# Differential attention, one head after another: v's transposes, norm sums and evictions placed one step later, and the ALiBi slopes moved from the bias table into q

## What is computed

```python
def diff_attention(q, k, v, lam, slopes):
    """q, k (b,s,h,2,d); v (b,s,h,e); lam scalar; slopes (h,).
    out_t = sum_s [softmax1 - lam*softmax2]_{ts} v_s, both maps with ALiBi."""
```

## Time and profile before

| | us |
|---|---|
| median of 3 runs | 4327.98 (4327.98 to 4328.1) |
| the profiled execution | 4328.54 |
| its span in the trace | 4326.8 |
| the attention stage in it, PE's first `av` to the last `ya` | 1778 to 2627, so 849 |
| from the first scores of head 1 to those of head 7 | 1928.4 to 2540.8: 612.4, or 102.1 a head |

### The profile page before, as it was taken

The page is one execution under the profiler, slowest core; times in us unless marked ns, Lnnn a source line. Parts: engine busy times, 40 slices in busy tenths (PEclk is TensorE's granted clock), DMA queues, the critical chain, the costliest instruction groups (busy, mean ns, idle before and its releaser), DMA issues.

```text
span 4326.8 us, 48830 instructions
## 1 busy us (share of the span) xinstructions
PE 3819.9 (88%) x20470; PEld 3154.3 (73%) x20470; DVE 2173.4 (50%) x2809; ACT 1657.8 (38%) x2217; POOL 528.7 (12%) x437
## 2 busy tenths in 40 slices
PE   6989999999987989788888877999888998879988
PEld 5768888787865777666666656977777777658988
DVE  3444343434464657355454443357777777732222
ACT  4323222121134555456566552144444444431122
POOL 0000011000002425000000000012222222200002
PEclk9989999999998989899999997999999999989999
DMA  2002021111111010100000004121111111142111
GB/s 87 30 25 79 30 73 46 42 49 49 49 50 40 30 40 20 49 25 25 25 25 25 25 17 158 40 75 33 40 39 40 35 49 44 47 178 78 40 40 64
DMA packets 196399, 211.31 MB, mean 49 GB/s; under 512 B 7944, under 2 KB 171733, under 8 KB 196181
## 3 DMA queue, kind: packets, MB, share of 16 engines
q1 hardware_dynamic: 190420, 187.22, 13.6%
q10 hardware_dynamic: 5760, 20.97, 1.2%
HBM read 174.62 MB, written 33.55 MB: 48 GB/s over the span
## 4 chain that ended last, share of the span: by engine, by line
PE 65%; DVE 16%; ACT 11%; issue 5%; DMA 2%; POOL 0%; SPq 0%; ACTq 0%; DVEq 0%; POOLq 0%
PE pd L211 56%; PE pq L211 7%; DVE t L2374 2%; ACT t L2322 2%; ACT t L311 2%; DVE t L320 2%; DVE t L2696 1%; PE pd L354 1%; PE pq L354 1%; DVE t L3099 1%; DVE t L2688 1%; DVE t L1785 1%; DVE t L2392 0%; DVE t L3084 0%; ACT L2358 0%
## 5 line engine op out<-in xcount | busy, mean ns | idle before, releaser
L211 PE MATMUL pd<-t 128*128 128x512 f32 (+2 forms) x15920 | 3132.6, 357 | 139.8 <-DVE t L599 43.4
L211 PEld LDWEIGHTS pd<-t 128*128 128x128 f32 x15920 | 2582.8, 193 | 628.6 <-issue 172.6
L211 PE MATMUL pq<-t 128*128 128x128 f32 (+5 forms) x3222 | 575.0, 341 | 155.2 <-DVE t L2374 37.7
L211 PEld LDWEIGHTS pq<-t 128*128 128x128 f32 (+2 forms) x3222 | 400.4, 186 | 286.7 <-issue 69.1
L311 ACT ACTIVATE t<-t 128x2048 fp32r<-128x2048 f32 (+2 forms) x134 | 241.6, 1804 | 754.1 <-PE pd L211 696.4
L320 DVE TENSOR_TENSOR t<-t 128x2048 fp32r<-128x2048 f32 (+2 forms) x134 | 295.5, 2206 | 385.9 <-ACT t L311 385.9
L354 PE MATMUL pd<-t 128*128 128x128 f32 x832 | 137.5, 318 | 108.6 <-DVE t L2392 32.3
L1385 DVE TENSOR_TENSOR t<-pd,t 128x512 f32<-128x512 f32 x256 | 171.6, 689 | 122.8 <-PE pd L211 122.8
L354 PEld LDWEIGHTS pd<-t 128*128 128x128 f32 x832 | 116.3, 165 | 134.9 <-DVE t L2392 32.1
L2322 ACT ACTIVATE t<-t 128x1024 f32<-128x1024 f32 x128 | 146.2, 1144 | 94.0 <-DVE t L2379 93.9
L2696 DVE SCALAR_TENSOR_TENSOR t<-t 128x1024 f32<-128x1024 f32 x120 | 178.6, 1488 | 0.3
(11 more groups left out here) (283 smaller groups left out, 2800.3 us busy)
## 6 DMA issues: line engine op xcount, KB each, us to landing
t<-in_w_in_dram SPq DMA_DIRECT2D x97, 512.0 KB, 4.9
t<-in_w_mlp_dram SPq DMA_DIRECT2D x32, 1024.0 KB, 5.3
t<-in_w_out_dram SPq DMA_DIRECT2D x20, 1024.0 KB, 5.1
t<-in_w_in_dram SPq DMA_DIRECT2D x16, 1024.0 KB, 5.4
t<-ym_scratch ACTq DMA_DIRECT2D x24, 512.0 KB, 7.2
t<-in_x_dram SPq DMA_DIRECT2D x16, 512.0 KB, 7.2
x_scratch<-t SPq DMA_DIRECT2D x16, 512.0 KB, 2.8
ym_scratch<-t SPq DMA_DIRECT2D x16, 512.0 KB, 2.6
```

Of the source, the lines that this page charges most:

```text
L211: ins = e.matmul(out, l, r, start=(first and j == 0), stop=(last and j == n - 1), skip_group_check=True)
```

## The change

There are two parts.

First, the slopes. `bias` is set once to -|distance|, and the factor goes to q: q's high and low parts are multiplied by 2^(h-2), and DVE's scores instruction scales by 2^-(h+1). Each is a power of two. L2316 is gone, and one multiplication at the stage's start is new.

Second, the order. The square comes ahead of the copy; the sum of squares, logarithm, exponential, gate and the write of a half are taken out of their place behind `AV` and put one or two tiles later (`*_att_ms`): the first half's at tile 4 (PE, ACT) and 5 (DVE, SP) of the head, the second half's at tile 0 and 1 of the next head. In `vg` both `av` come first, then `avT` with `ag` for each half. On ACT and DVE each eviction of `vg` and `qk` is one step later than the product. `tmp` has four tiles instead of two. `att_stage` spells out the weave with `vg` as a string of letters.

```diff
-    tmp = ring(ph, 2, [128, 512])
+    tmp = ring(ph, 4, [128, 512])
...
         for th in range(2):
             fm(e, u, 0, th, 2, "av", h, th)
             yield
+        for th in range(2):
             b = e.take(PD, "avT", h, th)
             e.wait_ge(*at["avc", h, th])
             transposed(e, b, [tmp.of("avc", h, th)[:, tile(j)] for j in range(4)]).then_inc(
                 *at.inc("pe", "avT", h, th, free=("avc", h, th)))
-            yield
-        for th in range(2):
             fm(e, u, 128, th, 2, "ag", h, th)
-            yield
-        pe_done(u)
+            if th == 1:
+                pe_done(u)
+            yield
+            yield
...
+    def owed(h, tt):
+
+        return (h, 0) if tt >= 4 else (h - 1, 1)
...
+    def act_att_ms(e, h, tt):
+        h, th = owed(h, tt)
+        if h >= 0:
+            q = tmp.of("osq", h, th)
+            e.wait_ge(*at["oms", h, th])
+            e.wait_ge(*at["epsc"])
+            e.activation(q[:, :], PD.of("oms", h, th)[:, :], ACT.Ln, scale=1.0 / 128, bias=epsc[:, 0:1]).then_inc(
+                *at.inc("act", "oln", h, th, free=("oms", h, th)))
+            e.wait_ge(*at["oln", h, th])
+            e.activation(q[:, :], q[:, :], ACT.Exp, scale=-0.5).then_inc(*at.inc("act", "ors", h, th))
...
-        e.mul(bias[:, :], bias[:, :], -4.0 if h == 0 else 0.5).then_inc(*at.inc("act", "bias", h))
...
-                next(a)
-                next(d)
-                weave((islice(a, 18), 18), (d, 5))
+                for who in "dada" "aaaaad" "aad" "aaaad" "ad" "aaaaa":
+                    next(a if who == "a" else d, None)
                 weave((a, 9), (qk(e, h + 1), 4))
```

More of the change, by code:

```diff
@@ L2177, in act_att_setup @@
         e.wait_ge(*at["dist"])
[L2178 removed]
+        e.activation(bias[:, :], bias[:, :], ACT.Abs).then_inc(*at.inc("act", "abs_dist"))
+        e.wait_ge(*at["abs_dist"])
+        e.mul(bias[:, :], bias[:, :], -1.0).then_inc(*at.inc("act", "bias"))
     def pe_att_vg(e, h):
@@ L2203, in act_att_vg @@
             e.copy(vT[:, :], PD.of("av", h, th)[:, :]).then_inc(*at.inc("act", "avc", h, th, free=("av", h, th)))
-            yield
+            if th == 0:
+                yield
+        for th in range(2):
             e.wait_ge(*at["avT", h, th])
@@ L2217, in act_att_vg @@
                 *at.inc("act", "agt", h, th, free=("ag", h, th)))
-            yield
+            if th == 0:
+                yield
+    QK4 = [(1, 0), (1, 1), (0, 0), (0, 1)]
     def pe_att_qk(e, h):
         u = pe_unit(e, W2in, [(2592 + h * 128, 128), (3616 + h * 128, 128)])
[L2222 to L2226, removed]
-    def act_att_qk(e, h):
-        act_unit(e)
[L2230 to L2242, removed]
@@ new lines, in pe_att_qk, with out_ @@
+        for m, th in QK4:
+            fm(e, u, m * 128, th, 2, "aqk", h, m, th)
+            if (m, th) == QK4[3]:
+                pe_done(u)
+            yield
+    def act_att_qk(e, h):
+        def out_(m, th):
+            sl, b = half(th), PD.of("aqk", h, m, th)
+            e.wait_ge(*at["aqk", h, m, th])
+            if h:
+                e.wait_ge(*at["scores", h - 1, 7, 1])
+            if m == 0:
+                e.mul(QS[0][LO, sl], b[LO, :], 2.0 ** (h - 2)).then_inc(*at.inc("act", "qk0", h, m, th))
+                e.mul(QS[1][HI, sl], b[HI, :], 2.0 ** (h - 2)).then_inc(*at.inc("act", "qkh", h, m, th))
+            else:
+                e.copy(KS[0][LO, sl], b[LO, :]).then_inc(*at.inc("act", "qk0", h, m, th))
+                e.copy(KS[1][HI, sl], b[HI, :]).then_inc(*at.inc("act", "qkh", h, m, th))
+                e.copy(KS[0][HI, sl], b[LO, :]).then_inc(*at.inc("act", "kc", h, th))
+                e.copy(KS[1][LO, sl], b[HI, :]).then_inc(*at.inc("act", "qkh", h, m, th))
+            at.also("act", ("aqk", h, m, th))
+        act_unit(e)
+        yield
+        for i in range(4):
+            out_(*QK4[i])
+            if i < 3:
@@ new lines, in dve_att_qk, with pe_att_ms @@
+        dve_unit(e)
+        yield
+        for i in range(4):
+            out_(*QK4[i])
+            if i < 3:
+                yield
+    def owed(h, tt):
+        return (h, 0) if tt >= 4 else (h - 1, 1)
+    def pe_att_ms(e, h, tt):
+        h, th = owed(h, tt)
+        if h >= 0:
+            b = e.take(PD, "oms", h, th)
+            e.wait_ge(*at["osq", h, th])
+            mms(e, b[:, :], [(ones[:, :], tmp.of("osq", h, th)[:, :])]).then_inc(*at.inc("pe", "oms", h, th))
+    def act_att_ms(e, h, tt):
+        h, th = owed(h, tt)
+        if h >= 0:
+            q = tmp.of("osq", h, th)
[5 more added lines that the diff above has]
+            e.activation(q[:, :], q[:, :], ACT.Exp, scale=-0.5).then_inc(*at.inc("act", "ors", h, th))
@@ L2262, in pe_att, with sp_att_ms @@
+    def sp_att_ms(e, h, tt):
+        h, th = owed(h, tt)
+        if h >= 0:
+            r = (8 + h) * 128
+            e.wait_ge(*at["oy", h, th])
+            e.dma(YM[r:r + 128, half(th)], AB[h % 2][0][:, half(th)], "ya", h, th)
     def pe_att(e, h):
@@ L2353, in act_att @@
                 e.wait_ge(*at["AV", h, th])
[L2354 to L2362, removed]
+                e.activation(q[:, :], b[:, :], ACT.Square).then_inc(*at.inc("act", "osq", h, th))
+                e.copy(o[:, :], b[:, :]).then_inc(*at.inc("act", "o", h, th, free=("AV", h, th)))
                 yield
```

94 lines of the change are left out of this document (49 added, 45 removed).

## The result

The changed kernel takes 4391.82 us (median of 4, 4386.6 to 4392.78) against 4328.04 for the kernel before in the same comparison: 1.0142 times as long, 95% interval 1.0124 to 1.0159. The forecast was 4396. The profiled execution took 4386.6, its span is 4384.8.

A forecast was written before the change was run, and what follows sets the result against it. PE, busy 88% of the span, was taken as the bound, so its idle time decides. Heads 1 to 6 add 63.6, head 0 +9.5, head 7 -3.6, prologue -1.4: together +68 on 4328.5, forecast 4396, range 4352 to 4424.

The forecast's parts named there:

- The first half of a head: From the previous head's last `AV` end to the next `AV` end: 66.9 against 53.95, +12.95.
- The walk: Step-through of the changed order with per-instruction prices, time 0 at an `AV` end; gave halves of 66.9 and 46.1.
- restart: PE's slowdown at the lower clock after an idle gap, priced at about 2.5 us.
- the second rival: Faster: if ACT reaches the second `avc` before PE's scores 3 end, first `avT` wait and restart vanish: 4316; chance 0.05.
- The second half: From the first half's `AV` end to the head's last: 46.1 against 48.5, -2.4, with 5.1 idle at `wT` 6.
- Head 0: Owes no norm, its Silu waits for no write: 108.9 against 99.4 before, +9.5.
- `avT` waits 6.7: In head 0's first half, PE's wait at the first `avT`, with exponentials 3 following maxima 3: 6.7 us.
- Head 7 and the prologue: Head 7, all chain without projections: -3.6; the prologue's two `avT` no longer wait a copy's length each: -1.4.
- rival 1: Waits come but cheaper, without restart cost: 4361, or 4348 if the write's landing also hid; chance 0.16.
- rival 4: Worse: third restart a head at the Silu wait and median landing of 2.8 add 3.3 a head: 4420; chance 0.10.
- Rival 3: No change: new waits only take the place of the 13 idle us a head: 4328; chance 0.03.
- the table loads: On ACT: 1.28 each without drain; the skill page's 1.38 drain per switch would put the sum some 17 higher.

The follow-up runs named there:

- the early `avc`: Changed kernel with one ACT statement moved: second `avc` right behind the first, not behind the exponentials of tile 3; 4344.5 us, 1.0034 of the kernel before.
- the slopes alone: Kernel before with only the first part of the change (slopes in q, old order); 4308.47 us, 0.9954 of the kernel before.
- two such moves and the early eviction: Changed kernel with second `avc` early, weight split under the first `AV`, second half's norm at the head's start; 4244.99 us, 0.9808 of the kernel before.
- early norm: Changed kernel with the norm of the previous head's second half moved to the head's start; 4345.06 us, 1.0038 of the kernel before.

## Why the prediction was right, point by point

**The first half of a head.** The walk gave 66.9, the trace 67.14. Its items: idle at the first `avT` 9.2, measured 9.12; restart 2.5, measured 2.7 (`avT` 1.12 instead of 0.6, `ag` 7.82 instead of 5.65); Silu waiting for the write some 3, measured 4.04; PE at `wT` 2 idle 1.60 and 2.09, together the 4.2 less 0.5 of the text, though only the 2.09 is the Silu's. That the sum comes within 0.24 is in part luck: the walk has scores 4 end at 44.8 where the trace has 44.0 (2424.50), and it has no restart behind the Silu's wait, where the trace has one of 1.8. The cause is shown by the early `avc`: with that one statement moved the wait at `avT` is gone.

**What the walk did not see.** It stopped at the buffer that `avT` takes. The buffer after it, which `ag` takes, was bound to the previous norm, and the long wait hid that. It made no difference to the forecast, but the second rival's price rested on it: "the 9.2 and its restart would fall away", 4316. With the early `avc` 4344.5 was measured.

**The second half.** 46.1 forecast, 45.5 measured; `wT` 6 idle 5.1 forecast, 5.58 measured; its restart 2.5 forecast, 3.0 measured (`wT` 1.97 instead of 1.03, projection 7.74 instead of 5.7); exponentials 6 begin 4.0 after the end of `AV` (2447.66, then 2451.65), as forecast.

**Head 0.** Forecast +9.5, measured +5.5: from about 1825.2 to 1930.11 is 104.9, not 108.9. The step that failed is "`avT` waits 6.7". Head 0 owes no `oms`, so the ring is one take behind: the first `avT` gets the buffer of the first `av` and does not wait, and the first `ag` waits for the second `avc`. This row of PE's timeline of the changed kernel shows it:

```profile
1849.18 1.06 PE L354 MATMUL pd<-t 128*128 128x128 f32 x4
1855.73 7.12 PE L211 MATMUL pd<-t 128*128 128x512 f32 x24 [5.48 <-ACT t L2207]
```

I had carried the ring over from the full heads without counting its takes again. What it cost at the lower clock was 1.5 (7.12 instead of 5.65), where 2.5 was forecast.

**Head 7 and the prologue.** From the last `AV` of head 6 to that of head 7 is 76.75 (2605.78 to 2682.53) where it was 81.93 (2539.06 to 2620.99): -5.2 for -3.6; the prologue gave 2.1 for 1.4. The errors of these small terms and of head 0 all have one sign: the stage's end moved by 61.5 in the trace (its last head's outputs are fetched from 2690.49 on, before from 2628.95), where 68 was forecast.

**The sum.** 66.9 + 46.1 against 67.14 + 45.50 decides it, since it counts six times. The median moved by 63.8, the forecast was 68; the span of the profiled execution moved by 58.0, less than its attention stage.

**The rivals.** The restart cost was paid at every long wait, so rival 1 falls. Of rival 4 one half came true: there is a third restart in each of heads 1 to 6, of 1.8 and not 2.5. The other half did not: all 16 writes of `ym_scratch` landed after 2.0. It had also priced seven heads, though head 0's Silu waits for no write. Rival 3 falls with the ratio of 1.0142: the new waits did not take the place of the old ones. Rival 2 falls by the rows, and the experiment that makes its condition true shows that even then the kernel would have been slower than before. On the table loads the row settles it: 2405.45 + 1.28, and the logarithm begins at 2406.74. The Trainium skill, page "ScalarE: Activation LUTs", section "What ACT_TABLE_LOAD costs", has a drain on top of each load; by the prediction's estimate from that page the sum would have been near 4413. The trace does not agree with it: no drain is seen here.

**What stays open.** The later stages are the same in both programs, but in the profiled execution they took 3.5 us less than before (61.5 against 58.0), and it ran 5 us below the other three; neither is explained. The price of a restart was read from rows (1.5 to 3.0 a time), not measured by an edit of its own. The clock's part of the gain of the slopes alone is read from the trace as well.

## What to carry to other kernels

When steps are delayed "by one" to give slack, count the takes of every small ring again, in the order of the engine that takes: the delayed reader may now hold the buffer that the producer wants next, and its real place in its own queue (here behind a norm and a tile of exponentials) is the wait. Put the helper work (weight splits, norms, writes) where its engine waits for the main one anyway; two such moves and the early eviction, a single statement, turned +64 us into -84. After the removal of a wait look at the ring's next buffer for the next one, and price the rest again.

## What the runs showed of the hardware that I had not expected

One and the same wait on PE has no fixed price. In the kernel before, in heads 2 to 6, a pair of waits of 2.7 was followed some 60 us later by one of 2.9, and the lower clock came behind the pair and behind the third. With the slopes alone the pair is 1.75 and 2.68 and the third wait is 2.94; in heads 2 to 6 the scores behind the pair are still slow, but behind the third wait the clock stays high. From the first `avT` of head 3 to that of head 4 is 98.92 (2142.30 to 2241.22), before 102.59 (2143.29 to 2245.88): 3.7 us shorter for 0.9 us less idle time at the first `avT`. Head 1 goes the other way: before, its third wait had no restart, and with the slopes alone it has one:

```profile
1941.64 0.66 PE L354 MATMUL pd<-t 128*128 128x128 f32 x4 [1.75 <-ACT t L2205]
1944.98 4.08 PE L211 MATMUL pq<-t 128*128 128x512 f32 x8 [2.68 <-DVE t L2382]
...
2008.89 1.74 PE L354 MATMUL pd<-t 128*128 128x128 f32 x8 [2.94 <-DVE t L2400]
```

So the 0.9 us alone does not decide it, and what does is not shown here.

Nor did a longer wait cost more. In the changed kernel the restart took 2.7 behind 9.1 us, 3.0 behind 5.6 and 1.8 behind 2.1; at the first `ag` it took 1.7 both behind 2.98 (early `avc`) and behind 6.25 (early norm).
